# GpSimd's order at the beginning of the up projections: crossed activations and weights in turn

## Chip, cores and metric

The kernel runs on one core of a Trainium2 chip. The metric is the device time of one execution in microseconds (us); less is better. One core has five engines with instruction streams of their own: TensorE (PE; its weight loads are listed as PEld), VectorE (DVE), ScalarE (ACT), GpSimd (POOL) and SyncE (SP), which here only issues transfers. They meet through semaphores.

## What is computed

Two transformer-like blocks over 512 tokens of width 1024, all in float32. What matters here is the feed-forward part that ends each of them, D_FF = 2816:

```python
h = rms_norm(x, norm2_g[layer])
gate, val = jnp.split(h @ w_up[layer], 2, axis=-1)
gate = jax.nn.silu(causal_depthwise_conv(gate, ffn_dw_w[layer], ffn_dw_b[layer]))
x = x + (gate * val) @ w_down[layer]
```

The second block has the same with `w_gate`, `w_up`, `conv_w`, `conv_b`, `w_down` and their `_2` arrays. Ahead of it the first block has attention and a convolution, the second a recurrence and sliding-window attention, each with an input and an output projection.

## The kernel before

**Products in high and low parts.** A float32 product is made of three matmuls on rounded numbers: high by high, high by low, low by high. So every weight tile passes through three hands. SyncE loads it into `w_raw` (four units of 128x1024, two slots by two). ScalarE copies it, rounded, into `w_hi` (`lead`, L806). Then GpSimd, or for some units VectorE, subtracts: `w_lo = w_raw - w_hi` (`rest`, L662 on GpSimd, L1368 on VectorE). `w_hi` and `w_lo` have four buffers each, by the unit's number modulo four. GpSimd's low parts count up `s_lo`, VectorE's `s_lod`; TensorE waits for them in `wait_lo` (L483).

**Units.** The weights of the kernel are numbered in the order of use. The first up projection begins at unit U_UP = 28, the second at U_UP2 = 154. In each, the first four units (28 to 31, 154 to 157) are ordinary ones, each the product of 128 output columns with all 512 tokens (`quad` on ScalarE and VectorE). After them come ten blocks of seven units, `sevenfold(i)`. Such a block computes 256 columns of the gate and 256 of the value with seven products of half size instead of eight, in the manner of Strassen and Winograd: sums of quarters of the weights times sums of quarters of the activations. On TensorE a product is 2 halves of 12 matmuls (L2374).

**Crossed activations.** Four of the seven products multiply sums of activations, `t1f` to `t4f`, which are the same for all blocks of a layer. VectorE makes them once (`cross`, L1576 to L1585), ScalarE rounds them (`cross_hi`, L1000, `s_th`), and GpSimd subtracts to get their low parts (`cross_lo`, L732, `s_tl`). They lie in the tile `tt`.

**Order in a layer's first block of seven** (units 32 to 38, and 158 to 164). Its products run in the order 1, 2, 0, 3, 4, 5, 6 (`FIRST_ORDER`, L127). The first two use plain activations. The third (product 0, unit 34) wants crossed part 1, the fourth (unit 35) crossed part 2, the sixth (unit 37) part 3, the seventh (unit 38) part 4: the waits on `s_tl` in `ready` (L2381, L2397, L2403, L2407). Units 35 and 36 are not loaded: VectorE adds them up from loaded quarters in `half_sum` (L1646 with unit 32's and unit 34's raw tiles, L1653 with unit 33's), into `sum_raw`. The low parts of units 35 and 37 are VectorE's (`on_vector`, L56), those of 32, 33, 34, 36 and 38 GpSimd's.

**What VectorE does around it,** in its own order: `cross` 1 to 4 with the norm's statistics between them (`spread`, L1395), a copy of the norm's factors (L1598), scaling and convolution taps of the quad on ScalarE's and its own operations (L1621, L1625, L1631), the two `half_sum`s, gating of the quad (L1621, L1671 twice), `rest(35)`, `rest(37)` (L1368), and the additions and taps of the block.

**What GpSimd does around it,** in its program's order: the sum of squares and the inverse root of the norm (L717, L702), the low part of unit 31, the four crossed low parts, then the low parts of units 32, 33, 34, 36, 38 and so on. Behind unit 32 (`sums_after`, from the table `SUMS_AFTER`) it issues one of the transfers of `block_sums` (L685), which prepare sums of weights in HBM for blocks much later; such an issue waits until the one before it has landed. In the second layer no such issues are left. The lines:

```python
            rests(U_UP + 3, 1)
            for x in range(1, 5):
                cross_lo(0, x)
            rests(U_UP + 4, U_IN2 + 2 - U_UP - 4)
```

**SyncE's loads.** A unit's load waits for the low part of the unit loaded four before it, and where a sum still needs that one's raw tile, for the sum (`one_block`, L561 to L573): unit 38's for L1646, unit 39's for L1653 and unit 33's low part, unit 40's for L1646 and unit 34's low part. ScalarE's `lead` of a unit waits until TensorE is through with the unit four before.

Of the kernel before, what the change touches and what calls it, by code (L numbers as in the profile page):

```python
# [35 lines left out]
U_IN, U_OUT, U_UP = 0, 20, 28  # L36
U_DOWN = U_UP + 4 * NC[0] + NB * NS[0]
U_IN2 = U_DOWN + KF
U_OUT2 = U_IN2 + 22
U_UP2 = U_OUT2 + 8  # L40
U_DOWN2 = U_UP2 + 4 * NC[1] + NB * NS[1]
U_END = U_DOWN2 + KF
TURN_BANK = (6, 7, 4, 5)
FIRST_BLOCK = (U_UP + 4 * NC[0], U_UP2 + 4 * NC[1])
# [11 lines left out]
def on_vector(u):  # L56
    at = block_of(u)
    return at is not None and at[1] in (3, 5)
# [130 lines left out]
def hybrid_blocks_kernel(  # L189
# [5 lines left out]
    with ExitStack() as ctx:  # L195
# [431 lines left out]
        def _(pool):  # L627
# [30 lines left out]
            def rest(at):  # L658

                pool.wait_ge(s_hi, at + 1)  # L660
                flat = is_flat(at)
                pool.tensor_tensor(unit_view(w_lo, at, flat), unit_raw(at, flat),  # L662
                                   unit_view(w_hi, at, flat).bitcast(F32), ALU.subtract).then_inc(s_lo, 1)

            def rests(u0, n):

                for u in range(u0, u0 + n):
                    if not on_vector(u):
                        rest(u)
                    sums_after(u)  # L670
# [23 lines left out]
            def sums_after(u):  # L694

                for _ in range(SUMS_AFTER.get(u, 0)):
                    block_sums(steps_done[0])
                    steps_done[0] += 1

            def inverse_root(n):  # L700
                pool.wait_ge(s_var, n)
                pool.tensor_tensor(rstd[:], stat[:], mhalf[:], ALU.pow).then_inc(s_rstd, 1)  # L702
# [9 lines left out]
            def add_squares(n, m):  # L712

                pool.wait_ge(s_sq, 8 * (n - 1) + m + 1)
                if m > 1:
                    pool.wait_ge(s_acc, 7 * (n - 1) + m - 1)
                pool.tensor_tensor(htmp[:, 0, :], htmp[:, 0, :], sq[:, m % 2, :], ALU.add).then_inc(s_acc, 1)  # L717

            def projected(n, u0):

                for m in range(6):
                    rests(u0 + m, 1)
                    if m:
                        add_squares(n, m)
                add_squares(n, 6)
                rests(u0 + 6, 1)
                add_squares(n, 7)

            def cross_lo(lay, n):
                x = (0, 1, 3, 2)[n - 1]  # L730
                pool.wait_ge(s_th, 4 * lay + n)
                pool.tensor_tensor(t_lo[x], t_f[x], t_hi[x].bitcast(F32), ALU.subtract).then_inc(s_tl, 1)  # L732

            projected(1, U_OUT + 4)
            inverse_root(2)
            rests(U_UP + 3, 1)
            for x in range(1, 5):
                cross_lo(0, x)
            rests(U_UP + 4, U_IN2 + 2 - U_UP - 4)
            for m in range(1, KD):  # L740
                add_squares(2, m)
            rests(U_IN2 + 2, 1)
# [34 lines left out]
            projected(3, U_OUT2 + 4)  # L777
            inverse_root(8)
            rests(U_UP2 + 3, 1)
            for x in range(1, 5):  # L780
                cross_lo(1, x)
            rests(U_UP2 + 4, U_DOWN2 - U_UP2 - 4)
            rests(U_DOWN2, 22)
            pool.wait_ge(s_gf, 16)
            for t in range(TT):
# [1920 lines left out]
```

## Time and profile before

| | us |
|---|---|
| median of 3 runs | 1179.99 |
| lowest, highest | 1179.94, 1180.92 |
| the profiled execution | 1179.95 |
| its span, first to last instruction | 1178.2 |
| TensorE's mean granted clock | 0.997 |

| engine | busy us | instructions |
|---|---|---|
| TensorE matmuls | 1149.7 | 7668 |
| VectorE | 827.9 | 1095 |
| ScalarE | 628.5 | 1007 |
| GpSimd | 619.5 | 316 |

The profiled execution gives all rows below; their times count from its first instruction. Busy time of an engine includes time in which an instruction has been started and is held up. Where it says "idle before", that is the time in which an engine waited, with the instruction that ended the wait.

### The profile page before, as it was taken

How to read it: one execution, taken by the hardware profiler on the slowest of the kernel's cores; microseconds unless marked ns; L12 is line 12 of the kernel's file. 1: busy time of each engine (PE TensorE's matmuls, PEld its weight loads, DVE VectorE, ACT ScalarE, POOL GpSimd, SP SyncE). 2: the span in 40 equal slices, each digit the busy share in tenths (PEclk: the TensorE clock that was granted, in tenths of full speed). 3: DMA queues.
4: the chain of work that ended last, by engine and by line, in shares of the span. 5: the costliest groups of instructions: out<-in, count | busy, mean ns of one | idle time of the engine just before them, and what ended most of it. 6: DMA issues, size and time to landing. Idle time of an engine off the chain costs nothing.

```text
span 1178.2 us, 19195 instructions
## 1 busy us (share of the span) xinstructions
PE 1149.7 (98%) x7668; PEld 995.2 (84%) x7668; DVE 827.9 (70%) x1095; ACT 628.5 (53%) x1007; POOL 619.5 (53%) x316
## 2 busy tenths in 40 slices
PE   7999999989999999999999999999999999999997
PEld 6877767779999999888877777778799999998886
DVE  5998974388888887544665577943868888875444
ACT  6346585545666565322455646656556565653323
POOL 3651132696767675544783210018867675755443
PEclk9999999999999999999999999999999999999999
DMA  5688771735866767636432211213245354442221
GB/s 185 236 224 220 191 210 19 187 105 199 202 205 200 200 217 216 196 130 159 118 109 80 72 37 38 74 36 108 74 123 145 110 148 121 144 142 81 100 90 72
DMA packets 110786, 162.64 MB, mean 138 GB/s; under 512 B 3587, under 2 KB 90986, under 8 KB 110698
## 3 DMA queue, kind: packets, MB, share of 16 engines
q1 hardware_dynamic: 97738, 115.02, 30.7%
q0 software_dynamic: 12800, 46.14, 15.9%
q8 instruction: 61, 1.00, 0.3%
q10 hardware_dynamic: 160, 0.26, 0.1%
q14 instruction: 27, 0.22, 0.1%
HBM read 159.05 MB, written 48.23 MB: 176 GB/s over the span
## 4 chain that ended last, share of the span: by engine, by line
PE 86%; DVE 6%; POOL 3%; ACT 3%; issue 1%; DMA 0%; POOLq 0%; ACTq 0%; DVEq 0%
PE ps L2374 34%; PE ps L2425 10%; PE ps L2429 10%; PE ps L2040 6%; PE ps L2041 6%; PE ps L2042 6%; PE ps L2129 4%; PE ps L2613 4%; PE ps L2175 1%; POOL htmp L717 1%; PE ps L2565 1%; PE ps L2160 1%; POOL w_lo L662 1%; DVE diag L1395 1%; DVE act_t L1585 1%
## 5 line engine op out<-in xcount | busy, mean ns | idle before, releaser
L662 POOL TENSOR_TENSOR w_lo<-w_raw,w_hi 128x1024 fp32r<-128x1024 f32 x176 | 458.9, 2624 | 246.5 <-ACT w_hi L806 245.1
L806 ACT ACTIVATE w_hi<-w_raw 128x1024 fp32r<-128x1024 f32 x210 | 220.9, 1054 | 198.3 <-PE ps L2429 77.2
L2374 PE MATMUL ps<-tt,w_hi 128*128 128x256 f32 x1280 | 232.4, 283 | 0.5 <-DVE w_lo L1368 0.3
L2374 PEld LDWEIGHTS ps<-tt,w_hi 128*128 128x128 f32 x1280 | 199.6, 192 | 0.9 <-DVE w_lo L1368 0.5
L2374 PE MATMUL ps<-tt,w_lo 128*128 128x256 f32 x640 | 181.1, 283 | 0.0
L1614 DVE TENSOR_TENSOR tt<-act_t,tt 128x512 fp32r<-128x512 f32 x44 | 99.1, 2259 | 101.7 <-ACT tt L1033 101.7
L2040 PE MATMUL ps<-h_hi,w_hi 128*128 128x512 f32 x376 | 153.0, 407 | 2.4 <-POOL w_lo L662 0.8
L2041 PE MATMUL ps<-h_lo,w_hi 128*128 128x512 f32 x376 | 147.0, 391 | 0.0
L2042 PE MATMUL ps<-h_hi,w_lo 128*128 128x512 f32 x376 | 146.8, 391 | 0.0
L2374 PE MATMUL ps<-h_hi,w_hi 128*128 128x256 f32 x440 | 124.6, 283 | 0.2 <-POOL w_lo L662 0.2
L2374 PE MATMUL ps<-h_lo,w_hi 128*128 128x256 f32 x440 | 124.5, 283 | 0.0
L2374 PE MATMUL ps<-h_hi,w_lo 128*128 128x256 f32 x440 | 124.5, 283 | 0.0
L2374 PEld LDWEIGHTS ps<-tt,w_lo 128*128 128x128 f32 x640 | 122.9, 192 | 0.0
L2425 PE MATMUL ps<-w_hi,tt 128*128 128x512 f32 x352 | 108.4, 389 | 0.0
L2429 PE MATMUL ps<-tt,w_hi 128*128 128x512 f32 x352 | 108.3, 389 | 0.0
L662 POOL TENSOR_TENSOR w_lo<-sum_raw,w_hi 128x1024 fp32r<-128x1024 f32 x20 | 48.1, 2407 | 103.0 <-ACT w_hi L806 103.0
L2040 PEld LDWEIGHTS ps<-h_hi,w_hi 128*128 128x128 f32 x376 | 70.7, 188 | 25.0 <-issue 7.6
L1368 DVE TENSOR_TENSOR w_lo<-w_raw,w_hi 128x1024 fp32r<-128x1024 f32 x34 | 66.0, 1945 | 30.1 <-ACT w_hi L806 30.0
L2374 PEld LDWEIGHTS ps<-h_hi,w_hi 128*128 128x128 f32 x440 | 84.5, 192 | 0.4 <-POOL w_lo L662 0.4
L2374 PEld LDWEIGHTS ps<-h_hi,w_lo 128*128 128x128 f32 x440 | 84.5, 192 | 0.0
L2374 PEld LDWEIGHTS ps<-h_lo,w_hi 128*128 128x128 f32 x440 | 84.5, 192 | 0.0
L2042 PEld LDWEIGHTS ps<-h_hi,w_lo 128*128 128x128 f32 x376 | 70.7, 188 | 15.4
(334 smaller groups left out, 2284.8 us busy)
## 6 DMA issues: line engine op xcount, KB each, us to landing
blocks<-in_w_up POOLq DMA_DIRECT2D x28, 1408.0 KB, 10.5
w_raw<-in_w_up SPq DMA_DIRECT2D x40, 512.0 KB, 3.6
w_raw<-blocks SPq DMA_DIRECT2D x40, 512.0 KB, 4.0
w_raw<-in_w_in SPq DMA_DIRECT2D x19, 1024.0 KB, 5.4
w_raw<-in_w_down SPq DMA_DIRECT2D x18, 1024.0 KB, 5.0
w_raw<-in_w_gate SPq DMA_DIRECT2D x20, 512.0 KB, 3.7
w_raw<-in_w_out SPq DMA_DIRECT2D x8, 1024.0 KB, 5.2
blocks<-in_w_gate POOLq DMA_DIRECT2D x4, 1408.0 KB, 7.3
```

The costliest lines, as they stand in the source:

```text
L662: pool.tensor_tensor(unit_view(w_lo, at, flat), unit_raw(at, flat), unit_view(w_hi, at, flat).bitcast(F32), ALU.subtract).then_inc(s_lo, 1)
L806: act.activation(unit_view(w_hi, at, flat), unit_raw(at, flat), ACT.Copy).then_inc(s_hi, 1)
L1368: dve.tensor_tensor(unit_view(w_lo, at, flat), unit_raw(at, flat), unit_view(w_hi, at, flat).bitcast(F32), ALU.subtract).then_inc(s_lod if ...
L1614: dve.tensor_tensor(lo, act_t[:, k, :], hi.bitcast(F32), ALU.subtract).then_inc(s_alo, 1)
L2040: pe.matmul(ps[:, bank, :], whi, hi, start=first, stop=False, skip_group_check=True)
L2041: pe.matmul(ps[:, bank, :], whi, lo, start=False, stop=False, skip_group_check=True)
L2042: mm = pe.matmul(ps[:, bank, :], wlo, hi, start=False, stop=last, skip_group_check=True)
L2129: mm = pe.matmul(ps[:, bank, :].rearrange("p (s n) -> p s n", n=P), a[:, k, t * P:(t + 1) * P], rhs, start=(k == 0 and n == 0), stop=(k == ...
L2374: mm = pe.matmul(ps[:, bank, 0:NH], weight[:, k, n], a, start=begin, stop=False, skip_group_check=True)
L2425: mm = pe.matmul(ps[:, bank, :], a[:, t * P:(t + 1) * P], w[:, cols], start=st, stop=False, skip_group_check=True)
L2429: mm = pe.matmul(ps[:, bank, :], w[:, m * P:(m + 1) * P], a, start=st, stop=False, skip_group_check=True)
L2613: mm = pe.matmul(ps[:, m % 4, :], w, a[:, at, :], start=(first and k == ks[0] and n == 0), stop=(last and k == ks[-1] and n == 2), skip_gr ...
```

## The change

GpSimd's program alone changes. In each layer, between the low part of the up projection's fourth unit and the rest of the layer, the four crossed low parts and the low parts of the first three units of the first block of seven are issued in turn. No operation is added or removed, and the other engines' programs are the same.

```diff
+            def first_parts(lay):
+
+                u = FIRST_BLOCK[lay]
+                cross_lo(lay, 1)
+                cross_lo(lay, 2)
+                rests(u, 2)
+                cross_lo(lay, 3)
+                rests(u + 2, 1)
+                cross_lo(lay, 4)
+
             projected(1, U_OUT + 4)
             inverse_root(2)
             rests(U_UP + 3, 1)
-            for x in range(1, 5):
-                cross_lo(0, x)
-            rests(U_UP + 4, U_IN2 + 2 - U_UP - 4)
+            first_parts(0)
+            rests(U_UP + 7, U_IN2 + 2 - U_UP - 7)
...
             rests(U_UP2 + 3, 1)
-            for x in range(1, 5):
-                cross_lo(1, x)
-            rests(U_UP2 + 4, U_DOWN2 - U_UP2 - 4)
+            first_parts(1)
+            rests(U_UP2 + 7, U_DOWN2 - U_UP2 - 7)
```

## Rows read from the trace of the kernel before

**Rows 1.** The page, part 4: the chain that ended last, shares by engine.
```profile
PE 86%; DVE 6%; POOL 3%; ACT 3%; issue 1%; DMA 0%; POOLq 0%; ACTq 0%; DVEq 0%
```

**Rows 2.** TensorE's timeline, 254 to 300: start, us, instruction [idle before it <- its releaser].
```profile
257.48 0.50 PE L2374 MATMUL ps<-f_first,w_hi 128*128 128x256 f32 x2 [2.83 <-POOL w_lo L662]
...
260.82 0.39 PE L2374 MATMUL ps<-h_hi,w_hi 128*128 128x256 f32 x1 [0.21 <-POOL w_lo L662]
...
264.17 0.51 PE L2374 MATMUL ps<-tt,w_hi 128*128 128x256 f32 x2 [0.21 <-POOL w_lo L662]
...
267.61 0.51 PE L2374 MATMUL ps<-tt,w_hi 128*128 128x256 f32 x2 [0.30 <-DVE w_lo L1368]
```

**Rows 3.** TensorE's timeline, second layer: first matmuls of the third and fourth products.
```profile
855.26 0.40 PE L2374 MATMUL ps<-tt,w_hi 128*128 128x256 f32 x2
...
858.14 0.40 PE L2374 MATMUL ps<-tt,w_hi 128*128 128x256 f32 x2
```

**Rows 4.** The chain that ended last, in order of time, 264 to 461: start, us, what.
```profile
264.66 2.91 DVE w_lo L1368
267.61 193.22 PE ps L2374 x1608
```

**Rows 5.** GpSimd's timeline, 243 to 264; overlapping rows come from different stretches.
```profile
243.21 2.84 POOL L732 TENSOR_TENSOR tt<-act_t,tt 128x1024 fp32r<-128x1024 f32 x1
...
243.21 6.18 POOL L732 TENSOR_TENSOR tt<-act_t,tt 128x1024 fp32r<-128x1024 f32 x2
...
249.34 3.41 POOL L732 TENSOR_TENSOR tt<-act_t,tt 128x1024 fp32r<-128x1024 f32 x1
...
255.08 2.35 POOL L662 TENSOR_TENSOR w_lo<-w_raw,w_hi 128x1024 fp32r<-128x1024 f32 x1
257.38 0.73 POOL L685 DMA_DIRECT2D blocks<-in_w_up  x1
258.13 5.99 POOL L662 TENSOR_TENSOR w_lo<-w_raw,w_hi 128x1024 fp32r<-128x1024 f32 x2
```

**Rows 6.** VectorE's timeline, 243 to 268.
```profile
243.72 3.41 DVE L1583 SCALAR_TENSOR_TENSOR act_t<-act_t 128x1024 f32<-128x1024 f32 x1
247.05 3.43 DVE L1585 TENSOR_TENSOR act_t<-act_t 128x1024 f32<-128x1024 f32 x1
...
257.22 1.29 DVE L1646 TENSOR_TENSOR sum_raw<-w_raw 128x1024 f32<-128x1024 f32 x1
258.55 3.31 DVE L1653 TENSOR_TENSOR sum_raw<-sum_raw,w_raw 128x1024 f32<-128x1024 f32 x1
...
262.57 0.69 DVE L1671 TENSOR_TENSOR act_t<-cv,ps 128x512 f32<-128x512 f32 x1
...
264.57 2.98 DVE L1368 TENSOR_TENSOR w_lo<-sum_raw,w_hi 128x1024 fp32r<-128x1024 f32 x1
```

**Rows 7.** VectorE's timeline, second layer: the same low part, with GpSimd idle.
```profile
852.84 1.22 DVE L1368 TENSOR_TENSOR w_lo<-sum_raw,w_hi 128x1024 fp32r<-128x1024 f32 x1
```

**Rows 8.** ScalarE's timeline: high parts of units 32 and 33.
```profile
252.59 1.05 ACT L806 ACTIVATE w_hi<-w_raw 128x1024 fp32r<-128x1024 f32 x1
...
255.64 1.04 ACT L806 ACTIVATE w_hi<-w_raw 128x1024 fp32r<-128x1024 f32 x1
```

**Rows 9.** The page, part 6: loads from the prepared sums, KB each, median us to landing.
```profile
w_raw<-blocks SPq DMA_DIRECT2D x40, 512.0 KB, 4.0
```

**Rows 10.** Busy time by stretch: PE, PEld, DVE, ACT, POOL; then clock, DMA share, GB/s.
```profile
254.60:257.50 2.90, 0.07 (x2) 0.02 (x1) 1.96 (x4) 2.54 (x4) 2.90 (x3) 1.00 0.03 6
837.50:839.50 2.00, 0.11 (x2) 0.06 (x2) 1.97 (x3) 0.68 (x1) 2.00 (x2) 1.00 0.00 0
839.70:843.00 3.30, 3.30 (x13) 2.91 (x12) 2.37 (x4) 1.90 (x3) 3.30 (x2) 0.50 0.00 0
```

**Rows 11.** Second layer: unit 159's high part on ScalarE, the first sum on VectorE.
```profile
843.92 1.05 ACT L806 ACTIVATE w_hi<-w_raw 128x1024 fp32r<-128x1024 f32 x1
...
845.51 1.30 DVE L1646 TENSOR_TENSOR sum_raw<-w_raw 128x1024 f32<-128x1024 f32 x1
```

## Prediction

> **What bounds the kernel now.** The page's shares of the chain that ended last say that TensorE has little slack: 86% of that chain is its own work [rows 1]. So a change on GpSimd can only count where TensorE waits. The next view is TensorE's waits after the output projection of the first block: four, all at the start of the first block of seven products, 2.83 + 0.21 + 0.21 + 0.30 = 3.55 us, three of them for a low part made by GpSimd (L662), the last for one made by VectorE (L1368) [rows 2]. After the last, at 267.61, the chain is TensorE alone for 193 us. The second layer has no such wait: its rows [rows 3] show TensorE going from product to product. So 3.55 us is all that the change can win.
>
> Which engine really sets 267.61? The chain of waits over that stretch is the third view [rows 4]. It is VectorE's for 24 us before it, with ScalarE's taps between: differences for the crossed activations, the first taps, the two sums of weights (L1646, L1653), gating, and the low part of the fourth product's weights (L1368), ready at 267.57. GpSimd's lateness at 257.4 is hidden behind that chain. Making GpSimd's low parts early wins nothing unless L1368 also comes earlier.
>
> The fourth view lays GpSimd beside VectorE [rows 5, 6]. A subtraction of 128x1024 on GpSimd takes 2.35 us alone (L662) but 3.41 where VectorE has an operation with two inputs in SBUF. VectorE's own 128x1024 operations take 1.22 alone [rows 7] and 3.31 to 3.43 beside GpSimd. The ends tell how: L1583 is asked for at 243.72, ends at 247.13, 1.1 us after GpSimd's first crossed part ended (246.05); the second crossed part ends at 249.39, 2.3 us behind L1583; L1585 ends at 250.48, 1.1 us behind that; the third crossed part at 252.75, 2.3 us behind L1585. The two take turns, whole instruction by whole instruction: 1.1 us for VectorE, 2.3 us for GpSimd. L1646, L1653 and L1368 do the same later. An operation with one input in PSUM (L1671, 0.69) keeps its time beside GpSimd. The Trainium skill (SBUF — State Buffer, "Who interferes with whom") states this as a rule: an exclusive lock between an operation with two SBUF inputs on VectorE and a reading one on GpSimd, held for the whole instruction by whichever issues first. The trace agrees. If the rows were read instead as two engines sharing a bandwidth, the forecast below would be the rival without the exclusion.
>
> **What the change does, first layer.** Nothing is added or removed. GpSimd's order was crossed parts 1, 2, 3, 4, then low parts of units 32, 33, 34, 36; it becomes 1, 2, 32, (one DMA issue), 33, crossed 3, 34, crossed 4, 36.
>
> Crossed parts 1 and 2 run as before and end at 249.39. Now GpSimd waits for the high part of unit 32, which ScalarE ends at 252.59 + 1.05 = 253.64 [rows 8]: GpSimd is idle for 4.3 us in which before it did crossed parts 3 and 4. VectorE gains nothing there, as L1585 had only waited for crossed part 2, and what follows it reads PSUM.
>
> Unit 32: 253.7 to 256.05, where before it ended at 257.43. The DMA issue, 0.73 us, until 256.8; it moves from 257.38 to 256.05, ahead of unit 33 as before. It stands beside an operation of VectorE in the trace and still takes 0.73; its transfer is read blocks later, so I cost it at nothing. Unit 33: its high part is there at 256.68, so 256.8 to 259.2.
>
> Here the price begins. VectorE comes to L1646 at 257.22, by its own chain, unchanged. Before it met the last 0.2 us of unit 32 and went ahead of unit 33, done at 258.51. Now unit 33 has held the pair since 256.8: L1646 waits until 259.2, ends 260.3 (+1.8). Crossed part 3: 260.3 to 262.6. L1653: until 263.7, before 261.86 (+1.8). Unit 34: 263.7 to 266.0, before 264.12 (+1.9). VectorE's four PSUM operations between, 2.7 us, bring it to L1368 at 266.4; at 266.0 crossed part 4 has taken the pair, until 268.4. L1368 ends at 269.5, before 267.57 (+1.9). Counted on GpSimd alone: four subtractions of 2.35, the issue and two turns of VectorE lie between 253.7 and unit 34's end, 12.3 us, which is 266.0.
>
> TensorE, at 2.88 us a product of 24 matmuls (855.26 to 858.14 in [rows 3]): the first from 256.1 to 259.0, the second 259.2 to 262.1, then idle until unit 34 at 266.05, and 268.95; then idle until L1368 at 269.5. Against 267.61 that is **+1.9 us**. The 1.3 us by which the first product starts earlier are lost in a wait of 3.9 us ahead of the third.
>
> Behind that, everything moved has slack. Unit 36 gets the pair at 269.5 and ends at 271.8, wanted at 272.4. Crossed parts 3 and 4 (262.6, 268.4) are wanted by the sixth and seventh products, after 275. SyncE issues the loads of units 38, 39 and 40 when L1646, L1653 and unit 34's low part are done: some 1.8 us later now, at 260.3, 263.7 and 266.0. Such a load lands in 4.0 us [rows 9], so by 264.3, 267.7 and 270.0, and ScalarE can't read them before their buffers of high parts are free, which is after products three, four and five, 268.9 or later. Cost nothing; without that cover it would be the 1.8 us once more.
>
> **The clock.** The trace has TensorE idle for 1.89 us at 837.5, and the granted clock is then 0.50 from 839.7 to 843.0, which is 1.2 instead of 2.4 GHz [rows 10]; a stretch of 3.4 us at half the clock costs 1.7 us of TensorE's work. After the 2.83 us at 254.6 the clock stayed at 1.00 [rows 2, 10], so no gap this short decides by itself. The new gap of 3.9 us is longer than both, and I take it that the clock falls near 266. Product three then takes 2.9 + 1.7 us, to 270.65, which covers the wait for L1368. TensorE starts product four at 270.65, **+3.0 us**. Bounds: 0 if it doesn't fall (+1.9), 1.7 on top of everything if it falls late (+3.6). I take +3.0, the full price from the nearest row, less what the wait for L1368 hides. The Trainium skill (TensorE: Matmul & The Clock Gate, "Why this matters for your kernels") tolerates longer idle gaps than the 1.89 us that was enough here; the measurement decides, and the new gap is too long by either.
>
> **Second layer.** No DMA issue here, and the turned transposes keep TensorE behind. By the same steps: unit 159's high part is there at 844.97 [rows 11], so GpSimd holds the pair until 847.45; L1646, asked for at 845.51 [rows 11], ends 848.5, crossed part 3 at 850.85, L1653 at 851.95, unit 160 at 854.3, wanted at 855.26; crossed part 4 at 856.7, L1368 at 857.8, before 854.06 [rows 7], wanted by product four at 858.14 [rows 3]. Hidden, with 0.3 us of slack. The low part of product five, again GpSimd's, follows at 860.1, wanted at 861.02. Price 0; if each turn were 0.1 longer, a few tenths.
>
> **Sum.** The profiled execution took 1179.95 us (span 1178.2), 0.04 under the median of the runs shown. 1179.95 + 3.0 + 0 = **1183.0 us**.
>
> **The rivals.**
> A, the forecast: turns at the pair, clock falls. For it: five encounters of the two engines in [rows 5, 6] all keep these turns. Chance 0.60; its own range +2.2 to +3.6.
> B, the clock holds through the 3.9 us gap, as it held through 2.83: +1.9, 1181.9 us. Chance 0.22.
> C, not slower: the exclusion doesn't reach L1646 and L1368 in the new order, because VectorE gets in beside or ahead of GpSimd. The place is unit 33 against L1646 at 257.2, the price 1.8 us. Freed of it, unit 34 ends at 253.7 + 9.4 + 0.73 = 263.8, product four starts at 266.7: -0.9, 1179.1 us. It decides from the point where L1653 ends before 261.9. Against it: L1653 and L1368 were both held up in the trace, and even with L1646 ahead of unit 33 the sum of turns on GpSimd stays 12.3 us. If TensorE's waits vanished wholly it would be 1176.4. Chance 0.08.
> D, worse: the second layer's 0.3 us of slack doesn't hold, or, with both waiting, GpSimd keeps the pair for two instructions and L1646 comes 2.3 us later still. Then +3.3 to +4.5, 1183.3 to 1184.5 us. Against it: no two of GpSimd's run past a waiting VectorE in [rows 5, 6]. Chance 0.10.
>
> **The numbers.** A difference under 0.2% (2.4 us) can't be told from none. A's mass lies mostly above that, 0.50 of 0.60; D's is all above: slower 0.60. B, the rest of A and the mild part of C: same 0.35. Faster needs a gain of over 2.4 of the 3.55 us: 0.05. The range takes in B and D: 1181.0 to 1184.5.
>
> **What would show it.** In the changed profile: unit 32's low part done near 256.1; L1646 at 2.9 to 3.1 us instead of 1.29; GpSimd idle some 4 us before 253.7; one wait of TensorE of nearly 4 us for L662 ahead of the third product; L1368 ending near 269.5; a stretch of 0.5 clock near 266; in the second layer, L1368 ending just before 858 plus the shift. I am wrong if L1653 ends by 262, or if the third product doesn't wait.

## The result, and the profile after

The changed kernel took 1183.26 us (median of 12 runs), the kernel before 1180.08 beside it (12 runs): a ratio of 1.0026, 95% interval 1.0019 to 1.0033, which is 3.1 us slower (the two medians alone differ by 3.2). The forecast was 1183.0, slower, with 0.2% as the bound.

| | before | after |
|---|---|---|
| span of the profiled execution, us | 1178.2 | 1181.7 |
| VectorE busy, us | 827.9 | 838.7 |
| GpSimd busy, us | 619.5 | 622.2 |
| TensorE's mean granted clock | 0.997 | 0.996 |

The number of instructions is the same on every engine. VectorE's busy time is up by 10.8 us, without a new operation: its operations last longer. In the new file the lines behind GpSimd's block are eight or nine higher: L1654 stands for L1646, L1661 for L1653, L1679 for L1671, L1376 for L1368, L2382 for L2374, L814 for L806. The experiments' files are shifted in the same manner, by up to 15 lines.

GpSimd's timeline after, 242 to 276, is the part to lay beside [rows 5]:

```profile
242.87 6.18 POOL L732 TENSOR_TENSOR tt<-act_t,tt 128x1024 fp32r<-128x1024 f32 x2
253.37 2.36 POOL L662 TENSOR_TENSOR w_lo<-w_raw,w_hi 128x1024 fp32r<-128x1024 f32 x1 [4.32 <-ACT w_hi L814]
255.68 0.73 POOL L685 DMA_DIRECT2D blocks<-in_w_up  x1
256.43 2.43 POOL L662 TENSOR_TENSOR w_lo<-w_raw,w_hi 128x1024 fp32r<-128x1024 f32 x1
258.80 3.42 POOL L732 TENSOR_TENSOR tt<-act_t,tt 128x1024 fp32r<-128x1024 f32 x1
262.18 3.33 POOL L662 TENSOR_TENSOR w_lo<-w_raw,w_hi 128x1024 fp32r<-128x1024 f32 x1
265.48 2.37 POOL L732 TENSOR_TENSOR tt<-act_t,tt 128x1024 fp32r<-128x1024 f32 x1
267.81 3.35 POOL L662 TENSOR_TENSOR w_lo<-sum_raw,w_hi 128x1024 fp32r<-128x1024 f32 x1
```

The idle time of 4.32 us in which crossed parts 3 and 4 ran before stands in the second row. Then unit 32, the DMA issue, unit 33, crossed part 3, unit 34 (done at 265.51), crossed part 4, unit 36. VectorE's timeline in the same stretch, to lay beside [rows 6]:

```profile
256.87 3.08 DVE L1654 TENSOR_TENSOR sum_raw<-w_raw 128x1024 f32<-128x1024 f32 x1
259.99 3.31 DVE L1661 TENSOR_TENSOR sum_raw<-sum_raw,w_raw 128x1024 f32<-128x1024 f32 x1
...
264.01 0.69 DVE L1679 TENSOR_TENSOR act_t<-cv,ps 128x512 f32<-128x512 f32 x1
...
266.01 2.92 DVE L1376 TENSOR_TENSOR w_lo<-sum_raw,w_hi 128x1024 fp32r<-128x1024 f32 x1
268.85 3.39 DVE L1376 TENSOR_TENSOR w_lo<-w_raw,w_hi 128x1024 fp32r<-128x1024 f32 x1
```

The first sum took 1.29 us before and takes 3.08: unit 33 was begun on GpSimd at 256.43, 0.44 us ahead of it. The last row, unit 37's low part, took 1.21 before and is now held up too. TensorE's timeline has two waits where [rows 2] has four:

```profile
255.78 0.50 PE L2382 MATMUL ps<-f_first,w_hi 128*128 128x256 f32 x2 [1.48 <-POOL w_lo L662]
265.56 0.80 PE L2382 MATMUL ps<-tt,w_hi 128*128 128x256 f32 x2 [3.52 <-POOL w_lo L662]
```

And the busy time by stretch (columns as in [rows 10]) shows the clock:

```profile
262.10:265.60 3.50, 0.04 (x1) 0.04 (x1) 3.29 (x5) 2.00 (x2) 3.50 (x3) 0.87 0.67 210
264.80:271.50 6.70, 5.94 (x28) 5.94 (x29) 6.60 (x4) 1.33 (x4) 6.36 (x3) 0.50 0.47 151
271.60:275.00 3.40, 3.40 (x31) 3.40 (x30) 3.40 (x4) 1.98 (x4) 2.40 (x1) 1.00 0.44 143
```

TensorE is busy for 5.94 us of the second stretch and gets through 28 matmuls at half the clock; behind it, 31 take 3.40 us.

**A ruler for all kernels.** The end of unit 31's product varies between executions (254.1 to 256.9 us here), since TensorE has waits further ahead that the change doesn't touch. Counted from that end, all is steady. It is the start of the first seven-fold product less the wait that stands in brackets: 257.48 - 2.83 = 254.65 before [rows 2], 255.78 - 1.48 = 254.30 after (where TensorE waits for nothing there, as in `high_early`, it is the end of unit 31's last matmul). The fourth product then starts at 267.61, that is 12.96 us behind it, before; and at 270.85, 16.55 us behind it, after. The difference, 3.59 us, is nearly the whole effect. In all twelve kernels of this study TensorE's timeline takes 31.7 to 32.1 us from the fourth product to the third block of seven (31.8 before, 32.0 after), 550.0 to 550.2 us from there to the first seven-fold product of the second layer, and 321.5 us from that to the end of its last matmul. The two profiled executions differ by 3.5 us of span: 3.6 and 0.2 less the 0.35 at the ruler's zero. The 0.2 belongs to the clock, which stays low into product four: where it doesn't fall (`first_filled`, below), the first of these stretches takes 31.8 as before, so SyncE's later loads of units 38 to 40 cost nothing.

### The profile page after: what moved, and what is told of

Read it like the earlier page. It is cut to its first block, busy times and chain, and to the rows that moved or that the text cites. A ratio compares the mean times of both kernels' runs of the same rounds, so it can differ in the third digit from the quotient of the medians.

```text
span 1181.7 us, 19195 instructions
## 1 busy us (share of the span) xinstructions
PE 1150.3 (97%) x7668; PEld 995.7 (84%) x7668; DVE 838.7 (71%) x1095; ACT 627.9 (53%) x1007; POOL 622.2 (53%) x316
## 4 chain that ended last, share of the span: by engine, by line
PE 86%; DVE 5%; POOL 4%; ACT 3%; issue 1%; DMA 1%; SPq 0%; POOLq 0%; ACTq 0%; DVEq 0%
PE ps L2382 34%; PE ps L2433 10%; PE ps L2437 10%; PE ps L2048 6%; PE ps L2049 6%; PE ps L2050 6%; PE ps L2137 4%; PE ps L2621 4%; PE ps L2183 1%; POOL w_lo L662 1%; PE ps L2573 1%; POOL htmp L717 1%; PE ps L2168 1%; DMA w_raw<-in_w_in 1%; DVE diag L1403 1%
## 5 line engine op out<-in xcount | busy, mean ns | idle before, releaser
L662 POOL TENSOR_TENSOR w_lo<-w_raw,w_hi 128x1024 fp32r<-128x1024 f32 x176 | 459.9, 2631 | 250.7 <-ACT w_hi L814 249.4
L814 ACT ACTIVATE w_hi<-w_raw 128x1024 fp32r<-128x1024 f32 x210 | 220.9, 1054 | 195.4 <-PE ps L2437 77.2
L2382 PE MATMUL ps<-tt,w_hi 128*128 128x256 f32 x1280 | 234.7, 285 | 3.5 <-POOL w_lo L662 3.5
L2382 PEld LDWEIGHTS ps<-tt,w_hi 128*128 128x128 f32 x1280 | 201.8, 194 | 3.7 <-POOL w_lo L662 3.7
L2382 PE MATMUL ps<-tt,w_lo 128*128 128x256 f32 x640 | 182.3, 285 | 0.0
L2382 PE MATMUL ps<-h_hi,w_hi 128*128 128x256 f32 x440 | 124.6, 283 | 0.0
L2382 PE MATMUL ps<-h_lo,w_hi 128*128 128x256 f32 x440 | 124.5, 283 | 0.0
L2382 PE MATMUL ps<-h_hi,w_lo 128*128 128x256 f32 x440 | 124.5, 283 | 0.0
L2382 PEld LDWEIGHTS ps<-tt,w_lo 128*128 128x128 f32 x640 | 124.1, 194 | 0.0
L662 POOL TENSOR_TENSOR w_lo<-sum_raw,w_hi 128x1024 fp32r<-128x1024 f32 x20 | 50.1, 2503 | 100.0 <-ACT w_hi L814 100.0
L1376 DVE TENSOR_TENSOR w_lo<-w_raw,w_hi 128x1024 fp32r<-128x1024 f32 x34 | 70.3, 2073 | 26.7 <-ACT w_hi L814 26.6
L2382 PEld LDWEIGHTS ps<-h_hi,w_hi 128*128 128x128 f32 x440 | 84.5, 192 | 0.2 <-POOL w_lo L662 0.2
L2382 PEld LDWEIGHTS ps<-h_hi,w_lo 128*128 128x128 f32 x440 | 84.5, 192 | 0.0
L2382 PEld LDWEIGHTS ps<-h_lo,w_hi 128*128 128x128 f32 x440 | 84.5, 192 | 0.0
```

The costliest lines, as they stand in the source:

```text
L814: act.activation(unit_view(w_hi, at, flat), unit_raw(at, flat), ACT.Copy).then_inc(s_hi, 1)
L1376: dve.tensor_tensor(unit_view(w_lo, at, flat), unit_raw(at, flat), unit_view(w_hi, at, flat).bitcast(F32), ALU.subtract).then_inc(s_lod if ...
L2382: mm = pe.matmul(ps[:, bank, 0:NH], weight[:, k, n], a, start=begin, stop=False, skip_group_check=True)
```

## The experiments

Theory T is the forecast's: the two engines take turns at a shared resource, instruction by instruction; the new order puts GpSimd first where VectorE was; VectorE's two sums, its gating and its low parts come later; and TensorE's gap costs it the clock. The rivals are named with each run. Every kernel ran 11 times, the kernel before 21 or 33 times beside it. Each ratio is to that kernel, with its 95% interval; it lies within 0.0002 of the ratio of the two medians, and the microseconds given are worked out from it. "Product four" is the start on the ruler above.

**Each layer alone.** In `first_only` the second layer keeps the old four lines; in `second_only` the first does.

```diff
-            first_parts(1)
-            rests(U_UP2 + 7, U_DOWN2 - U_UP2 - 7)
+            for x in range(1, 5):
+                cross_lo(1, x)
+            rests(U_UP2 + 4, U_DOWN2 - U_UP2 - 4)
```

> The new order in the first layer alone, the second as before. Theory T (the two engines take turns, which delays VectorE's low part of unit 35, and the clock then falls): all of the difference is made here, +3.0 to +3.6 us over before. Rival S (both layers pay, since in both L1646 and L1653 are held up): about half of it, +1.6. The trace should have the same wait of 3.5 us ahead of the third product and a stretch at half the clock behind it.

Measured: 1.0027 (1.0018 to 1.0036), 3.2 us slower. Product four at 16.52, the wait ahead of the third product 3.52 us, the clock at 0.50 from 266.9 for 6.8 us. Theory T holds. Rival S's half, +1.6, lies outside the interval.

> The new order in the second layer alone. Theory T: L1646 and L1368 take 3.0 us instead of 1.3 and 1.2, but unit 35's counterpart is ready 0.3 us before TensorE wants it: within 0.3 us of before. Rival S (both layers pay): +1 to +1.7.

Measured: 1.0002 (0.9993 to 1.0011), which by itself would leave room for the lower end of rival S; but in the trace the second layer takes TensorE 321.5 us as in every kernel, so S falls. The second layer is free, although its VectorE pays as the first's does. VectorE's timeline in `second_only`:

```profile
847.74 3.01 DVE L1655 TENSOR_TENSOR sum_raw<-w_raw 128x1024 f32<-128x1024 f32 x1
850.78 3.30 DVE L1662 TENSOR_TENSOR sum_raw<-sum_raw,w_raw 128x1024 f32<-128x1024 f32 x1
...
856.79 2.99 DVE L1377 TENSOR_TENSOR w_lo<-sum_raw,w_hi 128x1024 fp32r<-128x1024 f32 x1
```

Against 1.30 and 1.22 for the first and the third of them before [rows 7, 11]. They are held up, and TensorE doesn't wait for them: its only waits in that layer's beginning are those for the norm's factors and for ScalarE's copies of turned tiles.

**The clock by itself.** `first_filled` is `first_only` with matmuls that have no use in TensorE's gap, which keep it busy (`FILLERS` is 26). VectorE has one wait more, behind its low part of unit 37, so that it doesn't write into that part of PSUM too early:

```diff
+                    if first and lay == 0:
+                        dve.wait_ge(s_q, 5)
...
                         product(at, j, c)
+                    if first and lay == 0 and at == 1:
+                        for n in range(FILLERS):
+                            pe.matmul(ps[:, Y_BANK[0], NH:SEQ], h_hi[:, 1, 0:P], h_hi[:, 2, 0:NH], start=True, stop=True,
+                                      skip_group_check=True)
```

> As first_only, with 26 matmuls of 128x256 (26 x 0.12 = 3.1 us) put into TensorE's new gap behind the second product, on operands that are there and into a part of PSUM that is overwritten later; in the first block VectorE waits for the third product's first half before it writes there. They change nothing that is computed. Theory T with the clock as a term of its own: the clock stays at 1.00, product three takes 2.9 us, product four starts when VectorE's low part is ready: +1.9 us over before. Rival S2 (the clock costs nothing, since the wait for VectorE would follow anyway): the same as first_only, +3.0 or more.

Measured: 1.0012 (1.0003 to 1.0021), 1.4 us slower than before. The clock stays at 1.00; TensorE's timeline has the third product's start, then the fourth's, 14.75 us behind the end of unit 31's:

```profile
257.60 0.51 PE L2386 MATMUL ps<-f_first,w_hi 128*128 128x256 f32 x2 [1.47 <-POOL w_lo L663]
267.44 0.50 PE L2386 MATMUL ps<-tt,w_hi 128*128 128x256 f32 x2 [0.46 <-POOL w_lo L663]
270.88 0.51 PE L2386 MATMUL ps<-tt,w_hi 128*128 128x256 f32 x2 [0.31 <-DVE w_lo L1378]
```

So the 3.59 us fall into 14.75 - 12.96 = 1.79 for the turns and 16.55 - 14.75 = 1.80 for the clock. Rival S2 falls.

**Is it GpSimd that TensorE waits for?** The wait's name in the profile says so (`POOL w_lo L662`). `part3_early` puts crossed part 3 into GpSimd's idle time, so that its low parts of units 33 and 34 follow each other.

```diff
                 cross_lo(lay, 1)
                 cross_lo(lay, 2)
-                rests(u, 2)
                 cross_lo(lay, 3)
-                rests(u + 2, 1)
+                rests(u, 3)
                 cross_lo(lay, 4)
```

> First layer alone, GpSimd's order crossed parts 1, 2, 3, then units 32, 33, 34, then crossed part 4: part 3 fills GpSimd's idle time ahead of unit 32, and unit 34's low part is ready near 262.7, before the 264.1 of the kernel before. Theory T: L1646 is held up by unit 33, L1653 by unit 34 (ends 263.7), L1368 by crossed part 4 or unit 36 (ends 269.5 less the shift of the trace): product four starts 1.9 us later than before all the same, with TensorE's gap now ahead of it, and the clock can fall: +1.9 to +3.6 us. Rival G (TensorE waits for GpSimd's low parts, VectorE follows): unit 34 is 1.4 us earlier than before, so faster than before, -1.4 us.

Measured: 1.0012 (1.0003 to 1.0021), 1.4 us slower than before. Unit 34's low part was ready at 261.93 on GpSimd, 7.9 us behind unit 31's end instead of 264.12 - 254.65 = 9.5 before: earlier, and the kernel slower. Rival G falls. Product four started at 14.94, 1.98 us later than before, where T had 1.9. But the third product started at 10.50 with the gap ahead of it, and for a reason that neither theory had:

```profile
264.56 0.60 PE L2382 MATMUL ps<-tt,w_hi 128*128 128x256 f32 x2 [2.79 <-DVE act_t L1679]
```

The third product writes the bank from which VectorE reads the quad's value for its gating (L1671 in [rows 6]; `ready`, the wait on `s_gv`). VectorE's sums stand ahead of that gating, so it is late with them.

`part3_yield` adds that GpSimd waits behind unit 34 until VectorE's unit 35 is done:

```diff
                 rests(u, 3)
+                wait_lo(pool, u + 3)
+                rests(u + 3, 2)
                 cross_lo(lay, 4)
```

> As part3_early, but behind unit 34 GpSimd waits until VectorE's low part of unit 35 is done, then makes unit 36 and crossed part 4. GpSimd does the same work later. Theory T: L1368 takes 1.2 instead of 2.9 us and ends near 267.6 as in the kernel before; TensorE's gap ahead of product four shrinks to about 2 us: +0 us if the clock stays, up to +1.7 if it falls; some 1.9 us faster than part3_early. Rival G: not faster than part3_early, since GpSimd only waits more.

Measured: 1.0011 (1.0003 to 1.0020), the same as `part3_early`; product four at 14.89 against 14.94. Unit 35's low part took 1.22 us and ended 1.7 us earlier on the ruler (12.9 against 14.6), yet nothing came of it: the third product, at the low clock, was done later than either. The 1.9 us that I expected between the two didn't show, because the clock covers the turn. So both ran again with 20 useless matmuls (2.4 us) in the gap, and with the same wait on VectorE as in `first_filled`.

> As part3_early, with 20 matmuls (2.4 us) in TensorE's gap ahead of the third product, so that the clock stays at 1.00. Theory T: the third product waits for the gating and starts 10.5 us behind the end of unit 31's product, is done at 13.4, and then the fourth waits for L1368, which crossed part 4 or unit 36 has held up: 14.6. So product four hardly gains from the clock: 14.6 against 14.94 without the fill, and 12.96 before. Rival (only the clock delays product four): 13.4.

> As part3_yield, with the same 20 matmuls. Theory T: L1368 is not held up (1.2 us, done at 12.9), so the fourth product follows the third at 13.4: 1.2 us ahead of part3_early_filled, the price of one turn at the pair, and within 0.5 us of the kernel before at product four. Rival (whether L1368 is held up doesn't matter): the same as part3_early_filled.

Measured: 1.0016 (1.0007 to 1.0025) and 1.0009 (1.0001 to 1.0018). Product four at 14.75 and 13.48: 1.27 us apart. VectorE's timeline of `part3_early_filled`, and TensorE's:

```profile
267.04 2.98 DVE L1377 TENSOR_TENSOR w_lo<-sum_raw,w_hi 128x1024 fp32r<-128x1024 f32 x1
```

```profile
265.87 0.47 PE L2385 MATMUL ps<-tt,w_hi 128*128 128x256 f32 x2 [0.40 <-DVE act_t L1680]
270.08 0.51 PE L2385 MATMUL ps<-tt,w_hi 128*128 128x256 f32 x2 [1.11 <-DVE w_lo L1377]
```

and of `part3_yield_filled`, where the fourth product has no wait, VectorE's and GpSimd's:

```profile
266.55 1.22 DVE L1379 TENSOR_TENSOR w_lo<-sum_raw,w_hi 128x1024 fp32r<-128x1024 f32 x1
267.69 1.22 DVE L1379 TENSOR_TENSOR w_lo<-w_raw,w_hi 128x1024 fp32r<-128x1024 f32 x1
```

```profile
267.85 3.33 POOL L663 TENSOR_TENSOR w_lo<-sum_raw,w_hi 128x1024 fp32r<-128x1024 f32 x1 [5.11 <-DVE w_lo L1379]
```

GpSimd stands idle for 5.11 us, and product four starts earlier for it. In the whole time the gain isn't clear of the noise: the medians of the two kernels, 1182.25 and 1181.24 us, are 1.0 apart, and their intervals overlap. On the ruler it is the turn by itself: the low part came 1.8 us earlier (12.93 against 14.69), of which TensorE could take 1.27, until its third product was done.

**Who comes first.** `sum_first` takes `part3_early` and makes GpSimd wait for VectorE's first sum ahead of unit 33.

```diff
-                rests(u, 3)
+                rests(u, 1)
+                pool.wait_ge(s_sum, 1)
+                rests(u + 1, 2)
```

> As part3_early (first layer alone, crossed parts 1, 2, 3, then units 32, 33, 34, then crossed part 4), with one wait more: GpSimd begins unit 33 only when VectorE's first sum (L1646) is done. GpSimd's low parts of 33 and 34 come 1.6 us later than in part3_early. Theory T (what counts is which of the two gets to the shared pair first): L1646 takes 1.2 instead of 3.1 us, L1653 ends 1.8 us earlier, and with it the gating that the third product waits for and unit 35's low part: product four starts 13.0 us behind the end of unit 31's product, as in the kernel before, against 14.9 in part3_early. TensorE's one long gap becomes two short ones: within 0.3 us of before, or up to 1.7 above it if the clock falls. Rival G (TensorE waits for GpSimd): 1.6 us slower than part3_early, so +3 over before.

Measured: 1.0014 (1.0005 to 1.0024), 1.7 us over before. VectorE's timeline:

```profile
258.29 1.22 DVE L1656 TENSOR_TENSOR sum_raw<-w_raw 128x1024 f32<-128x1024 f32 x1
259.54 1.22 DVE L1663 TENSOR_TENSOR sum_raw<-sum_raw,w_raw 128x1024 f32<-128x1024 f32 x1
```

Both sums run unhindered (GpSimd, woken by the first, came 0.06 us after the second had begun). Unit 33 is late instead: TensorE waits 2.70 us for it, and the clock falls behind that wait:

```profile
260.40:263.00 2.60, 0.00 (x0) 0.00 (x0) 2.39 (x5) 1.78 (x4) 2.60 (x2) 1.00 0.99 387
263.70:267.00 3.30, 3.30 (x18) 3.30 (x17) 2.70 (x1) 0.00 (x0) 3.30 (x2) 0.50 0.82 234
```

Product four at 14.66, which is 1.7 above 12.96: the upper end of what T allowed. It is not later than in `part3_early`, although GpSimd's low parts are, so G fails here too; but as a test of the turn this run is worth little, the clock having taken what the turn gave.

**Does the kernel before pay for its own gap?** `before_filled` puts 22 of the same matmuls ahead of the first product.

> The kernel before with 22 matmuls of 128x256 (2.6 us) in TensorE's 2.83 us gap ahead of the first product, on operands that are there, into a part of PSUM that is overwritten later. Nothing that is computed changes. Theory C (the clock falls behind that gap in some executions of the kernel before, though not in the profiled one): the runs lie closer together and 0.3 to 0.6 us lower. Rival: no change, the 2.83 us gap never costs the clock.

Measured: 1.0000 (0.9991 to 1.0009), product four at 13.02. No gain; and yet the clock does fall behind that gap in some executions. `second_only` has the old order in its first layer, and its profiled execution shows it:

```profile
256.90:259.80 2.90, 0.10 (x2) 0.09 (x1) 1.96 (x4) 2.59 (x4) 2.90 (x3) 1.00 0.02 6
261.30:264.60 3.30, 3.30 (x17) 3.30 (x17) 3.30 (x2) 1.43 (x4) 3.30 (x2) 0.50 0.88 343
```

With these 3.3 us at half the clock, its fourth product still starts at 13.02, against 12.96 where the clock held. The slow products run in the time in which TensorE would have waited for GpSimd twice and for VectorE once (0.21, 0.21 and 0.30 in [rows 2]), at the end of which it has caught up. Theory C was wrong about the cost, not about the fall.

**A version faster than both.** If VectorE's chain sets the time and the idle seconds of GpSimd lie where the high parts are missing, the high parts must come earlier, and GpSimd must keep out of VectorE's way. `high_early` changes both engines, in the first layer alone:

```diff
+            def first_parts(lay):
+                u = FIRST_BLOCK[lay]
+                cross_lo(lay, 1)
+                cross_lo(lay, 2)
+                rests(u, 3)
+                pool.wait_ge(s_sum, 2)
+                cross_lo(lay, 3)
+                wait_lo(pool, u + 3)
+                rests(u + 3, 2)
+                cross_lo(lay, 4)
...
                 for x in range(1, 5):
+                    if x == 3 and not lay:
+                        lead(u0 + 4)
+                        lead(u0 + 5)
                     cross_hi(4 * lay + x)
...
-                        lead(u0 + 4 * i + 4 + c)
+                        if lay or c in (0, 3):
+                            lead(u0 + 4 * i + 4 + c + (2 if c == 0 and not lay else 0))
```

> First layer alone, three parts: ScalarE makes the high parts of units 32 and 33 ahead of the third crossed activation, and unit 34's where 32's was; GpSimd goes on behind crossed part 2 with units 32, 33, 34, waits for both of VectorE's sums, then crossed part 3, waits for VectorE's low part of unit 35, then unit 36 and crossed part 4. Theory T: unit 32's low part is there when unit 31's product ends (no gap, no fall of the clock), L1653 ends near 260.5, L1368 near 264.4, product four starts 10 to 10.5 us behind the end of unit 31's product instead of 13.0; up to 0.7 us is given back at the seventh product, whose low part now comes late: -1.8 to -3 us against before. Rival V (VectorE's chain can't be shortened by GpSimd's order): product four no earlier than before, 0 us.

Measured: 1177.95 us, 0.9980 (0.9971 to 0.9989), 2.4 us faster than the kernel before. Product four at 10.38 instead of 12.96, the clock at 1.00 from 240 to 300. GpSimd's timeline, then TensorE's only wait:

```profile
250.43 3.38 POOL L662 TENSOR_TENSOR w_lo<-w_raw,w_hi 128x1024 fp32r<-128x1024 f32 x1
253.76 0.73 POOL L685 DMA_DIRECT2D blocks<-in_w_up  x1
254.51 4.74 POOL L662 TENSOR_TENSOR w_lo<-w_raw,w_hi 128x1024 fp32r<-128x1024 f32 x2
261.68 2.41 POOL L732 TENSOR_TENSOR tt<-act_t,tt 128x1024 fp32r<-128x1024 f32 x1 [2.43 <-DVE sum_raw L1668]
265.62 3.33 POOL L662 TENSOR_TENSOR w_lo<-sum_raw,w_hi 128x1024 fp32r<-128x1024 f32 x1 [1.53 <-DVE w_lo L1383]
```

```profile
258.44 0.50 PE L2389 MATMUL ps<-f_first,w_hi 128*128 128x256 f32 x2 [1.28 <-DVE cv L1646]
```

The wait, the only one over 0.2 us between 240 and 300, is for VectorE's second tap of the quad, in the middle of the first product (L1646 in this file is L1631 of the kernel before, L1668 is L1653). The 0.7 us that I expected to lose at the seventh product didn't come: it starts 8.76 us behind the fourth, against 8.74 in the kernel before. Rival V falls. This order was not tried in the second layer, where there is nothing to win; and its parts were not run one by one, so which share is ScalarE's and which the two waits' stays open.

## Why the prediction was right

**The bound.** That the effect lies all in the first layer's first block is shown by `second_only` (nothing in the second layer) and `first_only` (all of it in the first). That VectorE's chain sets its end is shown by `part3_early` (unit 34 earlier, kernel slower) and by `part3_early_filled`, where the clock held and product four waited 1.11 us for VectorE's low part. 3.55 us as the most that can be won was not tested as a limit; the best order found wins 2.4.

**The turns, term by term.** From the end of unit 31's product, to take out the 0.35 us by which the two executions are apart there (254.65 and 254.30):

| ends | forecast | measured |
|---|---|---|
| unit 32's low part | 1.40 | 1.43 |
| L1646 | 5.65 | 5.65 |
| L1653 | 9.05 | 9.00 |
| unit 34's low part | 11.35 | 11.21 |
| L1368 | 14.85 | 14.63 |

Every encounter of the two engines went as in [rows 5, 6]. The forecast of +1.9 us for the turns alone, rival B's value, is what `first_filled` has at product four: +1.79. As a median it was +1.4, with 0.4 to 2.5 as the interval.

**The clock** was right in kind and short in size. I put it at 3.4 us of half clock, 1.1 us net of the wait for L1368. It lasted 6.8 us in both profiled executions with this order (`after` and `first_only`), and cost 1.80. Product three, from 265.56, ran wholly at the low level, 5.3 us instead of 2.9. The total, +3.6 on the ruler, lies at the upper bound that I had given for a late fall, but not by that route: the fall was early (264.7, inside the gap) and twice as long as the one that I had taken it from. In the medians, which take in executions where the fall begins elsewhere, it was +3.1; that part is inference, as only the profiled executions show where the clock falls. That the median came out within 0.3 us of the forecast is in part luck. On the ruler the forecast's +3.0 missed by 0.6: the turns took 0.1 less and the clock 0.7 more. In the medians the turns took about 1.4 (`first_filled`), where I had 1.9, and the clock the other 1.7, where I had 1.1, so that two misses would cancel; with intervals of 1 us either way that split is not settled.

**The second layer** cost 0, as forecast. Its margins were narrow, but wider than the 0.3 us of the forecast: L1368's counterpart ended at 861.04 there, and TensorE wanted it at 861.6 (858.14 in [rows 3], moved by the 3.5 us of all that follows). The fall of the clock in this layer, which stands in [rows 10], was missing in the profiled execution after the change; TensorE got nothing for it, since it then waited 1.32 us for ScalarE's copies:

```profile
852.02 1.11 PE L2323 MATMUL ps<-ident,xT 128*128 128x128 f32 x8 [1.32 <-ACT xT L1032]
```

**What the prediction missed.** The gating (L1671) as a release of the third product. In the changed kernel it came 0.8 us before unit 34's low part, ending at 264.70 against 265.51, so the miss did no harm. It misled me in `part3_early`, where I expected TensorE's gap ahead of the fourth product and found it ahead of the third.

**The rivals.** B was the right account of the turns without the clock, and `first_filled` is that kernel. C, that VectorE gets through: the first sum's 3.08 us rule it out, and L1653 ended at 9.00 on the ruler, above the 7.25 (261.9 in the trace of the kernel before) that I had set as the sign. D: neither of its two mechanisms appeared; no trace here has GpSimd running two instructions past a waiting VectorE.

## What to carry to other kernels

Before reordering an engine off the critical path, write down for each of its moved instructions which operation of another engine it will meet, and who will be first: here 0.44 us in the arrival decided 1.8 us. An engine off the critical path that is made to wait can help the one on it (5.11 us of idle GpSimd brought product four 1.27 us forward). And splitting several short waits of TensorE differently is not neutral, as one long gap also costs the clock; useless matmuls in the gap are a cheap way to measure that term by itself.

## What the runs showed of the hardware

The granted clock stayed at 0.50 for 6.8 us after a gap of 3.52 us, though TensorE was busy without a break from 265.56 on; after gaps of 2.70, 2.79 and 2.80 us (`sum_first`, `part3_early`, `second_only`) it was 3.4 us. After 2.83 us in the kernel before it didn't fall in the profiled execution, after 2.80 us in the same place in `second_only` it did: the length of a gap doesn't decide by itself. The second layer says the same of shorter ones: 1.89 us was followed by a fall in the kernel before [rows 10] and by none in `second_only`. And a fall can be free. In the first layer of the old order it moved product four by 0.06 us, in the second layer of any kernel here by nothing that the ruler shows, because other waits stood ready to take its place.
